# Gate and up products of ten feed-forward stages by Strassen's scheme, with the block sums on GpSimd

## What is computed

```python
def swiglu(x, w_gate, w_up, w_down):
    return (jax.nn.silu(x @ w_gate) * (x @ w_up)) @ w_down
# per stage: x = x + 0.5 * swiglu(rms_norm(x, g), w_gate, w_up, w_down)
# x: 256 x 1024; w_gate, w_up: 1024 x 2816; w_down: 2816 x 1024
```

## Time and profile before

| | |
|---|---|
| median of three runs | 3284.26 us |
| profiled execution, first to last instruction | 3282.6 us |
| TensorE busy | 3208.3 us (98%) |
| VectorE busy | 1832.9 us (56%) |
| ScalarE busy | 1529.3 us (47%) |
| GpSimd busy | 183.4 us (6%) |
| DMA engines, mean busy share | about 5 to 6 tenths, 176 GB/s |
| mean granted TensorE clock | 0.995 |

### The profile page before, as it was taken

The page is one execution under the profiler, slowest core; times in us unless marked ns, Lnnn a source line. Parts: engine busy times, 40 slices in busy tenths (PEclk is TensorE's granted clock), DMA queues, the critical chain, the costliest instruction groups (busy, mean ns, idle before and its releaser), DMA issues.

```text
span 3282.6 us, 38652 instructions
## 1 busy us (share of the span) xinstructions
PE 3208.3 (98%) x15901; PEld 2672.8 (81%) x15901; DVE 1832.9 (56%) x2426; ACT 1529.3 (47%) x1935; POOL 183.4 (6%) x297
## 2 busy tenths in 40 slices
PE   8999999979999999999999999999999999999998
PEld 6888888867888888878888888887788788977887
DVE  4467555475555475454575454665655655655545
ACT  4444444455444445444444443466544544565544
POOL 0000000022000000011000000012100000122000
PEclk9999999989999999999999999999999999999999
DMA  6555555523556555555556555654465555744553
GB/s 212 185 187 173 188 179 193 189 95 104 191 175 213 190 170 185 190 195 196 170 180 201 184 188 184 187 167 128 145 194 191 172 187 176 192 131 138 189 192 116
DMA packets 315851, 576.17 MB, mean 176 GB/s; under 512 B 45401, under 2 KB 114092, under 8 KB 315548
## 3 DMA queue, kind: packets, MB, share of 16 engines
q1 hardware_dynamic: 313148, 566.71, 53.7%
q0 software_dynamic: 2384, 6.64, 0.8%
q10 hardware_dynamic: 144, 0.35, 0.0%
HBM read 571.53 MB, written 1.09 MB: 174 GB/s over the span
## 4 chain that ended last, share of the span: by engine, by line
PE 87%; DVE 7%; ACT 4%; issue 1%; DMA 1%; POOL 0%; SPq 0%; DVEq 0%; ACTq 0%
PE up L1866 19%; PE up L1868 19%; PE up L1867 19%; PE acc L1866 8%; PE acc L1868 8%; PE acc L1867 8%; DVE w_lo L1073 3%; ACT w_hi L585 2%; PE up L2245 1%; DVE xT_lo L1189 1%; ACT xT_hi L659 1%; DVE x L1140 0%; ACT units L765 0%; PE acc L2470 0%; PE acc L1963 0%
## 5 line engine op out<-in xcount | busy, mean ns | idle before, releaser
L1073 DVE TENSOR_TENSOR w_lo<-raw,w_hi 128x2048 fp32r<-128x2048 f32 (+1 forms) x543 | 1234.5, 2275 | 1241.8 <-ACT w_hi L585 1239.8
L585 ACT ACTIVATE w_hi<-raw 128x2048 fp32r<-128x2048 f32 (+1 forms) x543 | 1034.0, 1906 | 1347.2 <-PE up L1868 963.2
L1866 PE MATMUL up<-w_hi,xT_hi 128*128 128x512 f32 (+1 forms) x2620 | 1027.2, 392 | 18.1 <-DVE w_lo L1073 6.8
L1868 PE MATMUL up<-w_hi,xT_lo 128*128 128x512 f32 (+1 forms) x2620 | 1019.7, 389 | 0.0
L1867 PE MATMUL up<-w_lo,xT_hi 128*128 128x512 f32 (+1 forms) x2620 | 1019.0, 389 | 0.0
L1866 PEld LDWEIGHTS up<-w_hi,xT_hi 128*128 128x128 f32 x2620 | 492.5, 188 | 126.3 <-DVE w_lo L1073 15.0
L1868 PEld LDWEIGHTS up<-w_hi,xT_lo 128*128 128x128 f32 x2620 | 492.7, 188 | 101.3
L1867 PEld LDWEIGHTS up<-w_lo,xT_hi 128*128 128x128 f32 x2620 | 492.9, 188 | 98.1
L1866 PE MATMUL acc<-w_hi,ff_hi 128*128 128x512 f32 x1232 | 487.3, 396 | 1.2 <-DVE ff_lo L1519 1.2
L1868 PE MATMUL acc<-w_hi,ff_lo 128*128 128x512 f32 x1232 | 480.3, 390 | 0.0
L1867 PE MATMUL acc<-w_lo,ff_hi 128*128 128x512 f32 x1232 | 479.6, 389 | 0.0
(11 more groups left out here) (319 smaller groups left out, 2292.7 us busy)
## 6 DMA issues: line engine op xcount, KB each, us to landing
raw<-in_ffn_down SPq DMA_DIRECT2D x88, 1024.0 KB, 4.9
raw<-in_ffn_gate SPq DMA_DIRECT2D x80, 1024.0 KB, 5.1
raw<-in_ffn_up SPq DMA_DIRECT2D x80, 1024.0 KB, 5.1
raw<-in_ffn_wi SPq DMA_DIRECT2D x80, 1024.0 KB, 5.2
raw<-in_ffn_wo SPq DMA_DIRECT2D x44, 1024.0 KB, 4.9
raw<-in_w_in SPq DMA_DIRECT2D x38, 1024.0 KB, 5.1
raw<-in_conv_w_in SPq DMA_DIRECT2D x24, 1024.0 KB, 5.1
raw<-in_w_in SPq DMA_DIRECT2D x44, 256.0 KB, 4.3
```

The lines of the kernel that those rows point to most:

```text
L585: nc.scalar.activation(w_hi[n % RING][:, 0:c], raw[n % RING][:, 0:c], ACT.Copy).then_inc(hi_ready, 1)
L1073: nc.vector.tensor_tensor(w_lo[n % RING][:, 0:c], raw[n % RING][:, 0:c], w_hi[n % RING][:, 0:c].bitcast(F32), ALU.subtract).then_inc(lo_re ...
L1866: pe.matmul(ps, lh, rh, start=start, stop=False)
L1868: return pe.matmul(ps, ll, rh, start=False, stop=stop)
```

## The change

Ten of the twelve feed-forward stages (all but those that follow tables part 0 and part 1) compute chunks 2 and 4 by the Winograd form of Strassen's scheme. A chunk is seen as a product of 2 x 2 blocks: the activations are split by token half and by half of the 1024 rows, the weights by half of the rows and by gate and up. Seven products of blocks (12 matmuls of 128 x 512 each) stand in place of eight.

- The products need four sums of activation blocks (`S_raw`, then `S_hi` and `S_lo`), once a stage, and four sums of weight blocks T1 to T4, once a chunk. GpSimd makes both (`fast_operands`, `fast_sums`). T1 = B11 + B12, T2 = T1 + B22, T3 = B12 + B22, T4 = B21 + T2, all of 128 x 2048 float32 and in place, in four new buffers `blocks` in the arena.
- For the activation sums the scaled activations are needed, so `rstd` is spread by a matmul at the start of the stage (`scale_done`, `scale_ready`), VectorE copies it to `rb`, and GpSimd adds hi and lo and multiplies by `rb` before it takes differences.
- A chunk's list is B11, spacer, B21, T1, spacer, B22, T2, spacer, T3, spacer, T4. The spacers are tiles of the old kind (down tiles, one tail tile) of 24 matmuls. So a fast chunk with its spacers has 11 entries of the ring in place of 8, and a stage has 39 in place of 33. `split_hi` and `split_lo` take the new ones from `blocks`.
- VectorE puts the seven products together (steps v, u, c12, c22, w, c21) and forms the two hidden halves.
- SyncE loads the blocks of a chunk in four DMAs of 1 MB ahead of their use, with waits for `scale_ready`, `S_summed`, `S_lo_ready` and `lo_ready` in its queue.
- `ple`'s DMA of p waits in addition for step w of the last fast chunk, since `S_hi` lies over its buffer.

The core of the diff:

```diff
+                def chunk(spacers):
+                    b11, b21, t1, b22, t2, t3, t4 = [(4, FW, None, name) for name in BLOCK_OF]
+                    return [b11, spacers[0], b21, t1, spacers[1], b22, t2, spacers[2], t3, spacers[3], t4]
+
+                t = wide(wg, 0) + wide(wu, 0) + wide(wg, 1) + wide(wu, 1) + chunk(downs[0:4])
+                t += wide(wg, 3) + wide(wu, 3) + chunk(downs[4:7] + [tail(0)])
+                return t + [tail(1)] + downs[7:11]
@@ SyncE
+                if j == 9:
+                    sp.wait_ge(scale_ready, seen.next(scale_ready))
+                    load_block(s, 2, 0)
+                    load_block(s, 2, 1)
+                elif j == 12:
+                    sp.wait_ge(S_summed, seen.next(S_summed, 4))
+                    load_block(s, 2, 2)
+                elif j == 15:
+                    sp.wait_ge(S_lo_ready, seen.next(S_lo_ready))
+                    load_block(s, 2, 3)
+                elif j == 22:
+                    sp.wait_ge(lo_ready, n0 + 18 + 1)
+                    load_block(s, 4, 0)
+                    load_block(s, 4, 1)
+                elif j == 24:
+                    load_block(s, 4, 2)
+                elif j == 27:
+                    load_block(s, 4, 3)
@@ VectorE, the start of a fast chunk (n is the entry of B11)
+                    consumed(n)
+                    hidden_lo(c - 1, 2)
+                    consumed(n + 1)
+                    consumed(n + 2)
+                    used()
+                    dve.wait_ge(p1_ready, seen.next(p1_ready))
+                    nc.vector.tensor_tensor(second, up[1][:], p1, ALU.subtract).then_inc(fast_step, 1)
+                    split_lo(n + 3 + RING)
+                    consumed(n + 4)
@@ TensorE
+                def fast(n, c, last_spacer):
+                    block_product(n, *x_block(0, 0), up[0][:], True)
+                    turn_hidden(c - 1, 4)
+                    if c == 2:
+                        pe.wait_ge(ff_lo_ready, seen.next(ff_lo_ready, 2))
+                    down(n + 1, c - 2, 0)
+                    pe.wait_ge(p1_ready, seen.next(p1_ready))
+                    block_product(n + 2, *x_block(0, 1), up[0][:], False)
+                    if c == 2:
+                        pe.wait_ge(S_lo_ready, seen.next(S_lo_ready))
+                    block_product(n + 3, *s_block(1), up[1][:], True)
+                    down(n + 4, c - 2, 1)
+                    pe.wait_ge(fast_step, base + STEPS_OF["v"])
+                    block_product(n + 5, *s_block(4), up[1][:], False)
+                    pe.wait_ge(ff_lo_ready, seen.next(ff_lo_ready, 2))
+                    block_product(n + 6, *s_block(2), up[2][:], True)
+                    down(n + 7, c - 1, 0)
+                    pe.wait_ge(fast_step, base + STEPS_OF["c12"])
+                    block_product(n + 8, *s_block(3), up[2][:], False)
+                    last_spacer(n + 9)
+                    block_product(n + 10, *x_block(1, 1), up[3][:], True)
@@ GpSimd
+            def fast_sums(n):
+                a, b, c, d = blocks
+                pool.wait_ge(block_in[1], seen.next(block_in[1], 16))
+                pool.wait_ge(lo_ready, n + 1)
+                pool.tensor_tensor(a, a, b, ALU.add).then_inc(sum_ready, 1)
+                seen.next(sum_ready)
+                pool.wait_ge(block_in[3], seen.next(block_in[3], 16))
+                pool.wait_ge(lo_ready, n + 3 + 1)
+                pool.tensor_tensor(a, a, d, ALU.add).then_inc(sum_ready, 1)
+                done = seen.next(sum_ready)
+                pool.tensor_tensor(b, b, d, ALU.add).then_inc(sum_ready, 1)
+                seen.next(sum_ready)
+                pool.wait_ge(sum_ready, done)
+                pool.wait_ge(lo_ready, n + 2 + 1)
+                pool.tensor_tensor(c, c, a, ALU.add).then_inc(sum_ready, 1)
```

More of the change, by code:

```diff
@@ L342, in build @@
         stored = sem("stored")
+        block_in = [sem(f"block_in{i}") for i in range(4)]
+        scale_done, scale_ready = sem("scale_done"), sem("scale_ready")
+        xs_step, S_summed, S_hi_ready, S_lo_ready = sem("xs_step"), sem("S_summed"), sem("S_hi_ready"), sem("S_lo_ready")
+        sum_ready = sem("sum_ready")
+        p1_ready, c11_gated, fast_step = sem("p1_ready"), sem("c11_gated"), sem("fast_step")
         def kpn(w):
@@ L377, in down_tile, with blocks_of @@
             return (2, D, [(slice(None), kpn(w[row:row + 2 * P, :]))])
+        fast_stages = [s for i, s in enumerate(plan) if s[0] == "ffn" and plan[i - 1] not in (("tables", 0), ("tables", 1))]
+        def blocks_of(s, c):
+            wg, wu, _ = ffn_weights(s)
+            return [kpn(w[512 * h:512 * h + 512, :])[:, :, FW * c:FW * c + FW] for h in range(2) for w in (wg, wu)]
         def tiles_of(s):
@@ L517, in build, with source @@
         n_tiles = count
-        used_cols = [nk * ncol for s in plan for nk, ncol, _ in tiles_of(s)]
+        every = [t for s in plan for t in tiles_of(s)]
+        used_cols = [t[0] * t[1] for t in every]
+        loaded = [n for n, t in enumerate(every) if t[2] is not None]
+        slot_of = {n: r % RING for r, n in enumerate(loaded)}
+        def source(n):
+            return raw[slot_of[n]] if n in slot_of else blocks[BLOCK_OF[every[n][3]]]
         def after(i):
@@ L540, in _, with slot_free @@
                           A["diff_subln_2"].rearrange("(o i) d -> o (i d)", o=1)).then_inc(gain_in, 16)
[L542 to L550, removed]
+            def slot_free(r):
+                if r >= RING:
+                    sp.wait_ge(lo_ready, loaded[r - RING] + 1)
@@ L551, in load @@
+            def load(r):
+                slot_free(r)
+                n = loaded[r]
+                nk, ncol, parts = every[n]
+                dst = tview(raw[slot_of[n]], nk, ncol)
                 for cols, src in parts:
                     rows, cols = cols if isinstance(cols, tuple) else (slice(None), cols)
-                    sp.dma_start(dst[rows, :, cols], src).then_inc(landed[n % RING], 16)
-            for s, n0 in zip(plan, first):
-                for j, t in enumerate(tiles_of(s)):
-                    load(n0 + j, t)
+                    sp.dma_start(dst[rows, :, cols], src).then_inc(landed[slot_of[n]], 16)
@@ L559, in _ @@
+            r = 0
+            for s, n0 in zip(plan, first):
+                for j in range(len(tiles_of(s))):
+                    if s in fast_stages:
+                        blocks_before(s, n0, j)
+                    if n0 + j in slot_of:
+                        load(r)
+                        r += 1
             if plan[-1][0] == "final":
@@ L582, in split_hi @@
                     return
-                act.wait_ge(landed[n % RING], seen.next(landed[n % RING], 16 * parts_of.get(n, 1)))
+                if n in slot_of:
+                    act.wait_ge(landed[slot_of[n]], seen.next(landed[slot_of[n]], 16 * len(every[n][2])))
+                elif every[n][3][0] == "T":
+                    act.wait_ge(sum_ready, seen.next(sum_ready))
+                else:
+                    b = block_in[BLOCK_OF[every[n][3]]]
+                    act.wait_ge(b, seen.next(b, 16))
                 c = used_cols[n]
-                nc.scalar.activation(w_hi[n % RING][:, 0:c], raw[n % RING][:, 0:c], ACT.Copy).then_inc(hi_ready, 1)
+                nc.scalar.activation(w_hi[n % RING][:, 0:c], source(n)[:, 0:c], ACT.Copy).then_inc(hi_ready, 1)
             def consumed(n):
@@ L1165, in _ @@
             starting = [True]
+            fast_chunks = [0]
             gated = []
@@ L2745, in _ @@
+            residuals, fast_chunks = 0, 0
+            for s, n0 in zip(plan, first):
+                if s in fast_stages:
+                    fast_operands()
+                    fast_sums(n0 + 8)
+                    fast_sums(n0 + 23)
+                    fast_chunks += 2
                 if s[0] == "mla":
```

278 lines of the change are left out of this document (271 added, 7 removed).

## The result

The changed kernel takes 3385.25 us, the median of four runs (3382.29 to 3386.23), beside 3284.65 of the kernel before: ratio 1.0304, interval 1.0291 to 1.0318. It is 100.6 us slower where 51 were forecast, and stands above the range that I gave. The profiled execution spans 3380.5 us.

The account below looks back on a forecast made before the run. TensorE, busy 98% of the span, was taken as the bound. From 3284.3 us, 47 us of gain and 98 us lost to VectorE's splits waiting on GpSimd's sums gave +51, 3335 us; range 3235 to 3362.

Parts of the forecast that it names:

- What goes and comes on TensorE: Fast stages: 54.4 us of block products go, 0.7 us a stage comes for spreading `rstd`; net gain 47 us.
- Turns between splits and sums: Fast chunks: VectorE's splits and GpSimd's sums, both with two SBUF inputs, alternate by whole instructions; TensorE loses 98 us.
- P: Time of one GpSimd sum of 128 x 2048, taken as 4.4 us; break-even for the change at 3.55 us.
- 3P - 8.3 a chunk: TensorE's lateness at the last two block products of each fast chunk, 20 times: 4.9 us each at the assumed P.
- the second transposes: Start of a fast stage, behind the activation sums and splits: little or no waiting forecast, zero cost.
- The clock: Rival: stalls in fast chunks each bring 3 us at half speed, 20 x 1.5 = 30 us, 3365 us; chance 0.04.
- the main case: Turns in the fast chunks with P from 3.8 to 4.8: 15 to 75 us slower, 3299 to 3360; chance 0.55.
- The faster rival (splits slip in): Fast chunks: GpSimd and VectorE hardly disturb each other, the 47 us gain stays, 3237 us; chance 0.26.
- The loads did not share: Rival at entry 22: six loads share the rate, up to 6 us late, up to 60 us more, 3395; chance 0.05.

Follow-up runs that it names:

- e1: The changed kernel with each of GpSimd's four weight-block sums cut to 8 of 2048 columns, output not the reference's: 3242.74 us.
- e2: The changed kernel with each GpSimd weight-block sum replaced by three fills of 128 x 2048 that read nothing, output not the reference's: 3245.02 us.
- e5: The changed kernel with each GpSimd weight-block sum cut into two instructions of 128 x 1024: 3308.02 us.
- e8: The changed kernel with only T3 of the four weight-block sums made by VectorE, the other three left on GpSimd: 3321.17 us.
- e6: The changed kernel with 5 and 11 empty fill matmuls on TensorE at the two waits of each fast chunk: 3359.56 us, ratio 1.0223 to the kernel before.
- e4: The changed kernel with T1 to T4 made by VectorE between its splits, activation sums left on GpSimd: 3251.18 us, ratio 0.9899 to the kernel before.

## Why the prediction was wrong

The direction and the mechanism were right, the size was not, and the measured time is above the range. By its steps:

- **What goes and comes on TensorE.** Reckoned -47 us. e1, which has all of the change but the block sums' size, gives 3242.74 - 3284.01 = -41.3. Right within 6 us; seven of the ten stages gain 4.3 to 4.5 in place of 4.7; one gains 1.5, with a low-clock stretch near 313 us that the kernel before does not have there. Some of the rest lies outside the fast stages: the one behind tables part 1 went from 192.28 to 194.55 us in e1 (195.38 in the changed kernel).
- **Turns between splits and sums.** Confirmed by e1 and e2 (the loss goes when the reads go), e5 (the unit is the instruction) and, more loosely, e8 (nearer to the schedule than to the amount of work, but 0.9 us a chunk above it).
- **P.** I took 4.4 us from rows that gave 3.6 to 4.2, and the sums took 4.62 undisturbed. The rows had a second input of one value per row; with two full operands 128 x 512 takes 1.29 us where that of the earlier trace rows took 1.05. So P was low by 0.2, which is 20 x 0.66 = 13 us by my own formula.
- **3P - 8.3 a chunk.** With P = 4.62 the formula says 5.6 a chunk, 111 us in all. e6, with the clock kept up, stands 3359.56 - 3242.74 = 116.8 above e1, and in that is 1.1 a stage at the second transposes (11.4 us), which I had put at zero: S_lo took 5.8 us behind T1's turn and pushed `product(1)`. Without it 105 us, 5.3 a chunk. The trace of the changed kernel says the same: its fast chunks without a low stretch take 5.5 us more than those of e1 (the second chunk of a stage) and 4.9 (the first, without the transposes). The formula holds.
- **The clock.** This is the step that failed. I gave 0.04 to a rival of 30 us, with the argument that stalls of 5 in 66 us are thin. So the sum had nothing for it. They are thin on average, but they come as one gap of 3.0 us close behind one of 1.1 to 1.5, and that was enough in 16 chunks of the 19 that have them. Measured: 25.7 us (e6), 1.5 us a place in the trace; the rival's price of 1.5 a stall was right, its chance and its place outside the sum were not. The granted clock in the earlier trace rows had shown that a stretch with gaps loses it. With the clock kept up, e6 takes 3359.56 us, just inside the range.

The measured terms: -41.3 (e1), 116.8 (e6 over e1), 25.7 (the changed kernel over e6). That they add up to the measured loss proves nothing, since each is the difference of two of the same times. A sum that could have failed goes by the trace: nine first chunks at 4.9 us over e1's, ten second ones at 5.5, the odd chunk at 8.4, 9.2 at the transposes of the other stages and 16 low stretches at 1.5 are 141, beside 139.6 us between the profiled spans of the changed kernel and of e1. Of the 50 us between forecast and result, some 26 are the clock, 13 P, 11 the transposes, 6 the gain, less about 6 that the formula had over what it gave.

The range failed with it: I had made the clock an alternative to the forecast, though it is a consequence. Where the forecast stalls TensorE, the clock's price belongs on top of it, in the main case.

The faster rival (splits slip in) fell, and what was said against its row fits: under GpSimd's tensor-scalars of the earlier trace rows, which read one input, the splits lost 0.09 and 0.19; under two-input sums they lose 3.7. No run varies the number of inputs alone, so that this is the reason stays likely and not shown. The loads did not share: the six issued from 600.62 us on landed in the order of their issue, 605.7 to 620.4, and entry 22's, the third, 7.1 us after its own issue, with no wait on DMA there. The Trainium skill's 4497 ns for the sum (GPSIMD Engine Reference, performance versus the Vector engine) was nearer to the measured 4625 than the carried-on rows were, and 3341 us by it would still have been 44 us short.

Left open: in e4 VectorE has some 18 us a stage more to do than in e1, and the waits for `ff_lo` that this brings fall in only five places; why there and not elsewhere I did not follow up. Open too is why three of the nineteen chunks kept the higher clock behind the same waits.

## What to carry to other kernels

Here work on GpSimd cost VectorE nothing where VectorE had at most one input in SBUF (step v) or where GpSimd only wrote (e2). Where both have two inputs there, reckon in turns: count how many GpSimd instructions can get in ahead of each VectorE instruction that something waits for, each for its whole length, and compare with the slack of that place, not of the stage. If such work must stay on GpSimd, cut it into short instructions, so that the turns in front of the critical instruction are short; better, ask first what it costs on VectorE (here half). And when a sum says that TensorE will stand still for about 3 us in one piece, add the lower clock behind the gap.

## What the runs showed of the hardware that I had not expected

- GpSimd's add of two full float32 operands of 128 x 2048 takes 4.62 us undisturbed; VectorE's takes 2.30.
- A wait of 3.0 us, some 3 us of matmuls behind one of 1.1 to 1.5, brought TensorE from 0.23 to 0.43 us between matmuls for the next 3 us or so in 16 places of 19, at 1.5 us each; 3.9 us of empty matmuls a chunk buy back 25.7 us of the whole. In e5, with no wait over 1.3 us at these tiles, the only low stretch in a fast chunk stands behind the 2.2 us wait of one stage's second transposes.
- GpSimd's fills of SBUF, 1.82 us each and back to back, cost VectorE's two-input splits nothing (2.34 us on average, with and without them).
- A plain float32 matmul of 128 x 128 takes some 0.23 us from start to start (11 of them take 2.62 us), as long as an fp32r one of 128 x 512.
